# B's gate and branch jobs all placed between the maps of C's attention, none behind B's own attention

## The reference

```
h = rmsnorm(x, norm_mix_g[l]) * (1.0 + sc1) + sh1
proj = h @ w_in[l]
xa_q, xa_kv, xb, xc, xd, gates = jnp.split(proj, splits, axis=-1)
y_a = mla_mixer(xa_q, xa_kv, ...)         # A, 8 heads
y_b = chunk_relbias_mixer(xb, ...)        # B, 8 heads
y_c = diff_mixer(xc, ...)                 # C, 4 heads, two maps each
y_d = swa_sink_mixer(xd, ...)             # D, 8 heads
ys = jnp.stack([y_a, y_b, y_c, y_d], axis=2)
branch = jnp.einsum('bsnw,nwd->bsnd', ys, w_branch[l])
gate = jax.nn.sigmoid(gates.reshape(b, s, N_BRANCH, d))
merged = jnp.sum(gate * branch, axis=2)
x = x + g1 * (merged @ w_out[l])
```

## Time and profile before

| | before |
|---|---|
| median of 3 runs | 2996.55 us (2994.24 to 2998.21) |
| profiled execution | 2994.19 us, span of its instructions 2992.6 us |
| PE busy | 2816.3 us, 94% of the span |
| DVE busy | 2115.6 us, 71% |
| ACT busy | 1653.0 us, 55% |
| mean granted TensorE clock | 0.975 |

### The profile page before, as it was taken

How to read it: one execution, slowest core, us unless ns; L and a number is a source line. 1 busy time by engine, 2 the same in 40 slices (tenths; PEclk the granted TensorE clock), 3 DMA queues, 4 the chain that set the end, 5 groups by cost and what they waited for, 6 DMA issues and landing times. The chain is left out here.

```text
span 2992.6 us, 44165 instructions
## 1 busy us (share of the span) xinstructions
PE 2816.3 (94%) x14520; PEld 2252.4 (75%) x14520; DVE 2115.6 (71%) x3015; ACT 1653.0 (55%) x2612; POOL 675.7 (23%) x563
## 2 busy tenths in 40 slices
PE   5999999999899999999789999999988999999995
PEld 4678777777678888888566777777776888888884
DVE  5544447555589999999845444565547989999997
ACT  2342434433368788888533334344324878888883
POOL 0100000100045753333210000000001557433330
PEclk9999999999899999999889999999999999999997
DMA  7224333333479999999722243433425999999995
GB/s 236 77 73 150 119 126 108 96 124 130 196 274 374 356 366 374 361 375 361 295 67 75 85 155 112 129 98 104 141 92 228 357 356 358 362 374 368 367 349 229
DMA packets 124560, 671.52 MB, mean 224 GB/s; under 512 B 27628, under 2 KB 29036, under 8 KB 90444
## 3 DMA queue, kind: packets, MB, share of 16 engines
q1 hardware_dynamic: 91040, 605.91, 55.3%
q0 software_dynamic: 31424, 57.44, 5.8%
q10 hardware_dynamic: 1932, 6.16, 0.9%
HBM read 656.60 MB, written 55.28 MB: 238 GB/s over the span
## 5 line engine op out<-in xcount | busy, mean ns | idle before, releaser
L2164 DVE TENSOR_TENSOR ew_lo<-ew,e_hi 128x2048 fp32r<-128x2048 f32 x258 | 591.3, 2292 | 96.0 <-ACT e_hi L1960 86.5
L712 PE MATMUL bank<-h_hi,w_hi 128*128 128x512 f32 x1248 | 509.3, 408 | 34.5 <-DVE w_lo L646 15.3
L1960 ACT ACTIVATE e_hi<-ew 128x2048 fp32r<-128x2048 f32 x260 | 498.4, 1918 | 13.7 <-PE bank L2379 7.3
L712 PE MATMUL bank<-h_hi,w_lo 128*128 128x512 f32 x1248 | 501.8, 402 | 0.0
L712 PE MATMUL bank<-h_lo,w_hi 128*128 128x512 f32 x1248 | 499.5, 400 | 0.0
L646 DVE TENSOR_TENSOR w_lo<-raw,w_hi 128x1024 fp32r<-128x1024 f32 x198 | 242.1, 1223 | 287.6 <-ACT w_hi L638 287.1
L2379 PE MATMUL bank<-e_hi,x_hi 128*128 128x512 f32 x1040 | 417.6, 402 | 0.1
L2379 PE MATMUL bank<-ew_lo,x_hi 128*128 128x512 f32 x1040 | 407.8, 392 | 0.0
L2379 PE MATMUL bank<-e_hi,x_lo 128*128 128x512 f32 x1040 | 405.4, 390 | 0.0
L1848 POOL DMA_INDIRECT y_d<-y,idx x130 | 218.5, 1681 | 476.0 <-issue 402.4
L712 PEld LDWEIGHTS bank<-h_hi,w_hi 128*128 128x128 f32 x1248 | 238.9, 191 | 112.1 <-issue 40.5
(11 more groups left out here) (337 smaller groups left out, 4930.4 us busy)
## 6 DMA issues: line engine op xcount, KB each, us to landing
ew<-in_wexp SPq DMA_DIRECT2D x130, 2048.0 KB
raw<-in_wmix SPq DMA_DIRECT2D x297, 512.0 KB, 3.6
ew<-in_wexp SPq DMA_DIRECT2D x130, 1024.0 KB
ew<-y_d SPq DMA_DIRECT2D x8, 2048.0 KB, 14.1
ew<-y_d SPq DMA_DIRECT2D x8, 1024.0 KB, 8.3
ada0a<-in_ada SPq DMA_DIRECT2D x2, 2048.0 KB, 13.6
ada0b<-in_ada SPq DMA_DIRECT2D x2, 2048.0 KB, 22.4
h_d<-htok ACTq DMA_DIRECT2D x8, 512.0 KB, 11.5
```

What stands on the lines that cost most here:

```text
L712: ins = nc.tensor.matmul(out, lhs, rhs, start=start, stop=stop)
L1960: nc.scalar.activation(e_hi[h][:], up_part(ew, j, h), ACT.Copy).then_inc(whi_done, 1)
L2164: nc.vector.tensor_tensor(up_part(ew_lo, j, h), up_part(ew, j, h), e_hi[h][:].bitcast(F32), ALU.subtract).then_inc(wlo_done, 1)
```

## The change

All sixteen jobs of `gbB` go between the maps of C's attention, ahead of D's projections. None is left alone behind B's attention. The order of the jobs and of their tiles stays.

```diff
         fill = {br: jobs[FILL[br]] for br in "ABCD"}
         alone = {br: jobs["gb" + br] for br in "ABD"}
-        held = len(jobs["gbB"]) // 2
-        fill["C"] = alone["B"][held:] + fill["C"]
-        alone["B"] = alone["B"][:held]
+        fill["C"] = alone["B"] + fill["C"]
+        alone["B"] = []
         shares = {br: spread(fill[br], NGROUP + 1) for br in "ABCD"}
```

## The result

The changed kernel takes 3008.18 us (median of 6 runs, 3004.31 to 3012.87) against 2995.16 us for the kernel before (6 runs, 2991.03 to 2998.21). The ratio is 1.0044, 95% interval 1.0031 to 1.0057: **slower**, by 9 to 17 us. The prediction said 2998.8, in a range of 2994 to 3004. The profiled execution is at the short end of the six, 3004.31 us.

The account below looks back on a forecast made before the run. TensorE, busy 94% of the span, was taken as the bound. Per layer +1.30 - 0.97 = +0.33, twice +0.66, plus 1.6 for the clock, gave +2.3 on 2996.55: 2998.8 us, range 2994 to 3004.

Parts of the forecast that it names:

- The boundary: Between B and C, the first bias waits behind four operations ending B's last set: hole 2.59 us for 1.29, +1.30 a layer.
- The middle of C: In C's slots, longer slots close the 0.97 us hole before the scores, -0.97 us a layer, and no new hole arises.
- The crowding that I named in slots 2 and 5: C's slots 2 and 5 hold two branch outputs each; slot 2's VectorE work, 8.3 us, exceeds the slot by 0.4; no hole.
- VectorE becomes late inside the slots: Rival in C's slots: bias queued behind splits comes late, 7 to 10 us a layer, about +16, 3013 us; chance 9%.
- The first slot's race: C's first slot: the second gate's weights must be split within it; ready 0.8 us early, so no cost.
- The clock: At C's start, a low-clock stretch in both layers; layer 2 already has it, layer 1 gets one, +1.6 us.
- a second stretch: Rival: a second low-clock stretch in each layer, 1.6 us more each, with the middle hole closed, 3002.0 us; chance 12%.
- Many small breaks: Rival in C's slots: moved products between breaks run at the low clock throughout, 66 us more, 3063 us; chance 1%.
- a middle hole of 0.97 a layer: Upper-bound case: the hole in the middle of C stays in both layers, +1.9 us.

Follow-up runs that it names:

- e6: The changed kernel with VectorE's low half of B's last set moved behind the bias of C's first two maps; 3000.98 us, ratio 1.0015 to the kernel before.
- e1: The changed kernel timed again, unaltered; 3006.2 us, ratio 1.0029 to the kernel before.
- e2: The changed kernel with two share boundaries shifted (slots 10 and 14 shorter, 11 and 15 longer), same jobs and order; 2998.01 us, ratio 1.0010.
- e5: The changed kernel, same shares, with gate 15's output (slot 10) and the split for D's last value job (slot 14) queued earlier; 2996.6 us, ratio 1.0006.
- e7: The kernel before with C's first two gate jobs (48 matmuls) moved from D's attention to the passage from C to D; 2982.93 us, ratio 0.9961.
- e8: All sixteen jobs of B in C, with the changes of e5, e6 and e7 together; 2977.42 us, ratio 0.9940 to the kernel before.

## Why the prediction was wrong

*The boundary* was right in mechanism and size: 2.60 us for 2.59, by the same four operations, and e6 showed for half of it that it is the queue.

*The middle of C* is the step that failed: the term that the prediction put at nothing measured 3.9 us a layer. It closed the 0.97 us hole, rightly, and then said "I take no hole there". It weighed VectorE's work against the length of a slot, and checked against it one demand of TensorE, the bias for the next scores. ScalarE didn't occur in it except as the maker of split halves. What TensorE also wants from a slot are the bank that an output frees and the weights of the next job. Both stand behind the exponentials in ScalarE's stream, and so behind VectorE's bias and in every fourth slot behind a set's norm. With shares of 17 or 18 no job in C waited for either; with shares of 25 or 26 two of them do. 1.58 + 2.35 us in each layer are 7.9 of the 10.3 us. The crowding that I named in slots 2 and 5 cost nothing.

*The rival "VectorE becomes late inside the slots"* had the sign and 9%. Its place, slots behind the sets' ends and slot 10, was nearly right. Its mechanism was not. Its condition was over 7.9 us of VectorE's work between two biases, twice in a row. In layer 1 of the changed kernel that work reaches 7.9 us in slot 2 and 8.0 in slot 5, each time with less behind it (6.1 us behind the second), and neither slot has a hole. By its own account it asked for seven holes a layer; there were two.

*The first slot's race* was harmless, as predicted.

*The clock* was half wrong. I took a low stretch at C's start in both layers. In four profiles with that 2.6 us hole (changed kernel, e1, e2, e5) two of eight were followed by one. The one in e2 lasted 6.8 us, so the rival "a second stretch" was real, but came in one place of the eight. What came instead stood behind slot 14's hole, 2.35 us: in both layers of the changed kernel, in one of e1, in none of e6. The account of the profiled execution is 2 x (1.31 - 0.97) = 0.7, plus 7.9 for the two holes, plus 2 x 1.6 for slot 14's echoes, less the 1.6 that layer 2 had paid at C's start before: 10.2 us, where B to D grew by 10.3. Its clock terms add up to 1.6 us, which is what I had predicted for the clock. That is luck: they come from slot 14, a place that the prediction didn't have.

*Many small breaks* was rightly out. e5 puts all 144 moved matmuls between breaks. B to D is 2 us shorter there than before, most of it the low stretch of before's layer 2 (layer 1 alone is 0.3 shorter), and the window over C's attention of layer 1 up to the hole at its end has the full clock:

```profile
410.00:541.00 131.00, 128.41 (x630) 100.43 (x626) 88.47 (x206) 54.19 (x135) 3.05 (x3) 1.00 0.36 125
```

The Trainium skill, page "TensorE: Matmul & The Clock Gate", section "A second HAM failure mode: psum-queue depth-cycling", tells of a kernel whose clock swung between its two levels because of frequent small idle times between groups of matmuls. The trace doesn't show that for the breaks of this kernel: over these 131 us its clock is 1.00. The page speaks of swings, so the 66 us that the prediction took from it, the low level throughout, are more than it states.

*The forecast of the total* was short by 7.8 us in the profiled execution (10.1 for 2.3), and the two holes are 7.9. (The medians of the first timing differ by 13.0, those of e1 by 11.1.) The range failed with it, since its upper bound kept a middle hole of 0.97 a layer, taken from the hole that I knew.

## What to carry to other kernels

When work is cut into equal shares and each engine follows the shares in its own in-order stream, list for every job what its start needs (bank, weights) and in which share the other engine delivers it. If that is the same share, the need stands behind everything else of that share, whatever it has to do with it; a small shift of the boundaries or one event moved up is then worth more than where the work lies. And work that stands alone between two dependent stages is not idle filler: at a passage where TensorE would wait for a chain over other engines it can be worth more than the same work spread between steps that are already covered (11 us of it a layer in e7).

## What the runs showed of the hardware

A hole of about 2.5 us is followed by a stretch at 1.2 GHz in some executions and not in others of the same kernel, with TensorE's hole the same to 0.01 us: behind C's start in one of two layers of e1 and none of the changed kernel. The two holes of 3.25 and 1.3 us between C and D come with one in both layers of all eight profiles that have them; it begins between 1.5 us before the end of the first hole and 1.3 us after it, and lasts 6.8 to 10.2 us. With the larger one covered (e7, e8) it was in none of four.
